# One layer step on one core: the prompt in one pass ahead of the expert gathers, or in groups of 256, 384 and 384 tokens beside them

## The reference, cut to what matters

```python
xn = rmsnorm(x, norm1_w)
q, c, kr, u_pool, gates = mixer_projections(xn, pos, p)   # xn @ w_in, latent norms, rope
attn = prompt_attention(q, c, kr, p)        # 8 heads of 96, causal, keys built from c and kr
# sample: sample_attention(...), online softmax over 32 pages of 128 cached rows per sequence
pool = pool_mix(u_pool, S, p)               # causal means over 2, 4, 8, 16 tokens, then a linear map
mixed = sigmoid(g0) * (attn @ w_attn_br) + sigmoid(g1) * (pool @ w_pool_br)
h = x + mixed @ w_out
y = h + peer(rmsnorm(h, norm2_w), p)
# peer: per token and each of 8 heads, scores against 2 x 128 keys, the best 16 of 16 x 16 sums;
# a = gelu(xn2 . u[e]) for the 128 chosen experts e, y = sum gate * a * v[e]   (u, v: 16384 x 1024)
```

## Time and profile before

| | |
|---|---|
| median of 3 runs | 4643.17 us (4634.75 to 4645.33) |
| profiled execution, its own time | 4673.63 us |
| its span, first to last instruction | 4671.8 us |
| TensorE busy | 3692.4 us, 79% |
| VectorE busy | 2738.3 us, 59% |
| ScalarE busy | 998.0 us, 21% |
| GpSimd busy | 2470.3 us, 53% |
| DMA, all queues | 1306.94 MB |
| first gather | at 1505 us |

### The profile page before, as it was taken

How to read it: one execution, slowest core, us unless ns; L and a number is a source line. 1 busy time by engine, 2 the same in 40 slices (tenths; PEclk the granted TensorE clock), 3 DMA queues, 4 the chain that set the end, 5 groups by cost and what they waited for, 6 DMA issues and landing times.

```text
span 4671.8 us, 47213 instructions
## 1 busy us (share of the span) xinstructions
PE 3692.4 (79%) x13481; PEld 1607.9 (34%) x13481; DVE 2738.3 (59%) x6886; ACT 998.0 (21%) x2045; POOL 2470.3 (53%) x2234
## 2 busy tenths in 40 slices
PE   8998787999998577777877778777878767676556
PEld 4433565444454233333333333333333323230001
DVE  3334331001104878878888888887878765666643
ACT  1121332001200224223323323322322310200000
POOL 0001100000000777777777777777777776677776
PEclk9998878999999788888888888888887878777778
DMA  2002002111323999999999999999999999999999
GB/s 105 1 28 36 2 0 95 41 40 59 109 63 101 361 388 381 396 380 388 396 394 388 388 399 396 392 396 386 396 396 389 374 405 412 386 407 390 372 372 382
DMA packets 441801, 1306.94 MB, mean 280 GB/s; under 512 B 90218, under 2 KB 146923, under 8 KB 438707
## 3 DMA queue, kind: packets, MB, share of 16 engines
q0 software_dynamic: 313344, 1140.99, 62.6%
q1 hardware_dynamic: 128242, 163.51, 10.7%
HBM read 1275.49 MB, written 28.75 MB: 279 GB/s over the span
## 4 chain that ended last, share of the span: by engine, by line
POOL 28%; DMA 14%; PE 11%; issue 10%; DVE 3%; SPq 2%; ACT 1%; DVEq 0%; ACTq 0%; POOLq 0%
POOL arena L1280 28%; DMA arena<-in_peer_v,arena 9%; PE ps_m L1343 4%; PE ps_m L1591 3%; DMA arena<-in_cache_krope 2%; DMA arena<-key_scores 1%; SPq L1544 1%; DMA arena<-in_peer_u,arena 1%; DVE arena L1385 1%; PE ps_m L1581 1%; PE ps_m L1616 1%; PE ps_m L1599 1%; SPq L1542 1%; PE ps_m L1600 1%; PE ps_m L1932 0%
## 5 line engine op out<-in xcount | busy, mean ns | idle before, releaser
L1343 PE MATMUL ps_m<-arena 128*32 128x512 f32 x4352 | 1171.3, 742 | 584.0 <-DMA arena<-in_peer_v,arena 558.3
L1385 DVE CUSTOM_DVE_ANT_0 arena<-arena 128x1024 f32<-128x1024 f32 x1088 | 1318.6, 1225 | 523.1 <-DMA arena<-in_peer_u,arena 491.5
L1280 POOL DMA_INDIRECT arena<-in_peer_u,arena x1088 | 1207.9, 1110 | 639.6 <-issue 329.0
L1280 POOL DMA_INDIRECT arena<-in_peer_v,arena x1088 | 1200.4, 1103 | 403.3 <-issue 306.9
L1343 PEld LDWEIGHTS ps_m<-arena 128*32 128x32 f32 x4352 | 193.8, 120 | 1346.2 <-DMA arena<-in_peer_v,arena 921.5
L1591 PE MATMUL ps_m<-arena 128*128 128x512 f32 x1056 | 567.7, 664 | 2.6 <-ACT arena L1671 2.4
L1581 PE MATMUL ps_m<-const,arena 128*128 128x128 f32 x528 | 135.7, 346 | 177.7 <-DMA arena<-in_cache_krope 148.8
L1591 PEld LDWEIGHTS ps_m<-arena 128*128 128x128 f32 x1056 | 202.5, 213 | 196.9 <-issue 190.5
L1671 ACT ACTIVATE arena<-ps_m 128x512 f32<-128x512 f32 x264 | 158.2, 599 | 514.5 <-PE ps_m L1591 510.0
L944 POOL COPY arena<-arena 128x1024 f32 (+1 forms) x8 | 8.3, 1042 | 489.4 <-POOLq L821 407.4
L1663 ACT ACTIVATE arena<-ps_m 128x256 f32<-128x256 f32 x264 | 101.4, 384 | 689.7 <-PE ps_m L1582 688.7
(11 more groups left out here) (235 smaller groups left out, 4465.4 us busy)
## 6 DMA issues: line engine op xcount, KB each, us to landing
arena<-in_cache_ckv SPq DMA_DIRECT2D x256, 128.0 KB
arena<-in_w_merge SPq DMA_DIRECT2D x16, 1536.0 KB, 9.2
arena<-in_w_peer SPq DMA_DIRECT2D x32, 576.0 KB, 4.1
arena<-in_peer_u,arena POOLq DMA_INDIRECT x1088, 7.6
arena<-in_peer_v,arena POOLq DMA_INDIRECT x1088, 7.6
arena<-key_scores SPq DMA_DIRECT2D x68, 128.0 KB, 10.8
key_scores<-arena SPq DMA_DIRECT2D x32, 256.0 KB, 4.5
arena<-in_w_front SPq DMA_DIRECT2D x1, 4864.0 KB, 18.9
```

Of the source, the lines that this page charges most:

```text
L1280: self.nc.gpsimd.indirect_dma_start(out=ring[:, slot, :], out_offset=None, in_=self.I[table], in_offset=bass.IndirectOffsetOnAxis(ap=self. ...
L1343: mm = self.nc.tensor.matmul(self.acc[32 * j:32 * j + 32, n, :], self.diag[:, (q0 + j) // 16 % DIAGS, (q0 + j) % 16, :], self.v_ring[:, (q ...
L1385: self.nc.vector.tensor_tensor_reduce(out=u, in0=u, in1=self.xrep[jg % self.XBUF], scale=1.0, scalar=0.0, op0=ALU.mult, op1=ALU.add, accum ...
```

## The change

The build keeps one block of instructions. The 1024 prompt tokens are cut into three groups of 2, 3 and 3 tiles of 128 tokens (`GROUPS_OF`). Each engine runs all stages of the first group (with the 64 sample tokens, 320 columns) first; `Now` gives them no slots. Then the gathers start, and the second and third group (384 columns each) are put between the slots by `Main`. Where each piece goes is computed by `Plan`: each piece has an estimated TensorE time, a group has a rate (estimated us per slot, the smallest that lets its scores be ready for `Route`), and `at` and `after` turn a piece into a slot. By its arithmetic group 1 takes the slots from 0 to 197 at a rate of 2.65 and group 2 those from 199 to 432 at 2.4. Page groups start at slot 442, one every 6 slots, the sample tokens' merge at 856, and its last scores are stored by slot 941; SLOTS stays 1108.

```diff
+GROUPS_OF = (2, 3, 3)
-PAGES_AT, PAGE_SLOTS = 16, 12
+PAGE_SLOTS = 6
...
+            pr.sync(Now(sp), groups[0], groups[1])
+            main = Main("SP", sp, ex.sync(sp))
+            for g, following in zip(groups[1:], after[1:]):
+                pr.sync(main, g, following)
+            pg.sync(main)
+            sm.sync(main)
...
+    rate, unit = 2.4, H * tile
+    while True:
+        g = Group(i, tile, tiles, base, rate)
+        if g.half_at <= route_slot(unit) and g.done_at <= route_slot(unit + 4):
+            return g
+        rate += 0.05
...
+    def piece(self, name, us, lead=0):
+        if self.base is None:
+            return
+        self.t += lead
+        self.begin[name] = self.t
+        self.t += us / self.rate
+        self.end[name] = self.t
```

In `Experts`, all four waits for v rows are moved ahead of the products:

```diff
+                for j in range(w):
+                    pe.wait_ge(self.v_in[(q0 + j) % RING], 16 * ((q0 + j) // RING + 1))
                 for n in range(2):
                     for j in range(w):
-                        if n == 0:
-                            pe.wait_ge(self.v_in[(q0 + j) % RING], 16 * ((q0 + j) // RING + 1))
                         mm = self.nc.tensor.matmul(self.acc[32 * j:32 * j + 32, n, :], ...
```

In `Pages`, a page is one transfer of 1152-byte rows from an array that holds both caches, the five steps of a group stand one slot apart, the exponentials stand behind the last page's square, and the weighing stands last:

```diff
-            for cols, src in ((slice(0, KL), "cache_ckv"), (slice(KL + 1, PGW), "cache_krope")):
-                sp.dma_start(self.pages[par][:, j, cols], self.I[src][ds(page, 1)].rearrange("a p c -> (a p) c")).then_inc(self.page_in[par], 16)
+            sp.dma_start(self.pages[par][:, j, 1:PGW], self.I["cache"][ds(page, 1)].rearrange("a p c -> (a p) c")).then_inc(self.page_in[par], 16)
...
             for j in range(5):
-                pe = main.to(slot + 1 + 2 * j)
+                pe = main.to(slot + 1 + j)
                 if gi < DB * GROUPS and j < n:
                     if j + 1 < n:
                         self.transposes(pe, j + 1, at, par)
                     self.keys(pe, j, at, gi, b)
-                if gi and j == 0:
-                    self.spread_maxima(main.to(slot + 2), gi - 1)
-                if gi and j == 2:
+                if gi and j == 1:
+                    self.spread_maxima(pe, gi - 1)
+                if gi and j == 4:
                     self.weigh(pe, self.group(gi - 1)[3], gi - 1, 1 - par)
...
-                if gi and j == 1:
+                if gi and j == 3:
                     self.correct(act, gi - 1)
                     self.exponentials(act, self.group(gi - 1)[3], gi - 1)
```

More of the change, by code:

```diff
@@ L137 @@
[L137 to L147, removed]
-LATT = ATS - 2 * H * NS
-LATE = LATT - 2 * N_IDS
-QT = TOP - H * TOK
-KT = QT - H * TOK
-CT = KT - 2 * TOK
@@ new lines, in _, with route_slot, paced @@
+            pr.vector(Now(dve), groups[0])
+            main = Main("DVE", dve, ex.vector(dve))
+            for g in groups[1:]:
+                pr.vector(main, g)
+            pg.vector(main)
+            sm.vector(main)
+            main.finish()
+def route_slot(unit):
+    return TOPK * (unit - 5) + 4
+def paced(i, tile, tiles, base):
+    if base is None:
+        return Group(i, tile, tiles, None, 1.0)
+    rate, unit = 2.4, H * tile
[4 more added lines that the diff above has]
+        rate += 0.05
+        assert rate < 20
@@ new lines, with __init__, to, finish @@
+class Main:
+    def __init__(self, name, eng, program):
+        self.name, self.eng, self.program, self.at = name, eng, program, 0
+    def to(self, slot):
+        while self.at < slot:
+            next(self.program)
+            self.at += 1
+        return self.eng
+    def finish(self):
+        for _ in self.program:
+            pass
+class Now:
+    def __init__(self, eng):
+        self.eng = eng
+    def to(self, slot):
+        return self.eng
+class Plan:
+    def __init__(self, base, rate):
+        self.base, self.t, self.rate, self.begin, self.end = base, base, rate, {}, {}
+    def piece(self, name, us, lead=0):
[5 more added lines that the diff above has]
+        self.end[name] = self.t
+    def at(self, name, part=0.0):
+        if self.base is None:
+            return 0
+        return int(self.begin[name] + part * (self.end[name] - self.begin[name]))
+    def after(self, name, more=0):
+        if self.base is None:
+            return 0
+        return int(self.end[name]) + 1 + more
@@ new lines, in act_scores @@
+    def act_scores(self, main, g):
+        s, ps, i, T = self.nc.scalar, self.ps, g.i, g.T
+        for j in range(2 * H):
+            n = 16 * i + j
+            if g.first and j >= 10 and j % 2 == 0:
+                self.rt.softmax(main.to(0), j // 2 - 5)
+            act = main.to(g.after(f"s{j}") - 1)
+            act.wait_ge(self.q_done, n + 1)
+            if j >= 2:
+                act.wait_ge(self.k_done, n - 1)
+            s.activation(self.qb(g, j % 2), ps[:, 2 + j % 2, 0:T], ACT.Copy).then_inc(self.q_out, 1)
@@ L1798, in vector @@
     def vector(self, main):
-        main.to(PAGES_AT)
+        main.to(self.first)
         self.start_batch()
```

2217 lines of the change are left out of this document (1205 added, 1012 removed).

## The result

The changed kernel takes 4725.82 us (median of 4 runs, 4721.13 to 4750.06) where the kernel before takes 4644.25 (4 runs beside it, 4634.75 to 4660.01): a ratio of 1.0183, with an interval from 1.0137 to 1.0228. The forecast was 4695 us and slower; the range was 4370 to 4980. The profiled execution took 4721.1 us with a span of 4719.1.

The account below looks back on a forecast made before the run. TensorE bounds the front and transfers the rest, in balance with a closed page loop that would bind after the change; 405 + 1560 + 1978 + 335 + 448 = 4726 us of span, 4695 us as median, range 4370 to 4980.

Parts of the forecast that it names:

- front: Work before the gathers: 312 us of TensorE work and 93 us that no work covers, 405 us (370 to 440).
- first groups: Slots 0 to 442, prompt groups 1 and 2: gathers plus reread weights plus 3%, 1560 us (1450 to 1860).
- pages: Slots 442 to 852: 64 page groups at 30.3 us, new rows and first load, 1978 us (1790 to 2220).
- The factor to the median: Step from profiled span to median of the runs: 0.9935, taking 4726 us to 4695 us.
- The sign: Whole kernel: slower, 4695 against 4643 us; faster 0.39 with A and B, slower 0.56 with C.
- rival C: Slots 0 to 442: prompt groups fall behind at 4.2 us a slot, 1856 us there, 4990 us in all; 20%.
- The page loop: Page stage: closed loop of 21.8 us to the weighing's end, 0.8 and 7.7 of load, 30.3 us a group.
- half-rate restart: First keys of each page group after the DMA wait: low clock, 3.41 us against 1.72, penalty 1.7 us a group.
- The four waits: Waits for second rows ahead of the products, 272 blocks: up to 54 us lost or 40 gained, taken as 0.
- Rival D: Expert product blocks: the wait for four rows is what counts, 54 us either way at most; no chance given.
- A: Whole kernel: transfers bind throughout at a DMA share of 1.01, median 3860 us; 5%.
- B: Page stage: the loop closes in 25 us, pages landing 5 us after first issue, median 4340 us, faster; 17%.

Follow-up runs that it names:

- the first experiments: Changed kernel with TensorE's waits for second rows back between the products, 4803.1 us; kernel before with all four waits ahead of the products, 4877.92 us.
- the changed kernel with the waits between: Changed kernel with TensorE waiting for each second row just before its own product, not for all four ahead: 4803.1 us, on another chip 4718.05 us.
- the last version: Changed kernel with three page buffers, maxima one slot later, page numbers read before the wait, second-row waits between products, exponentials before the last page's square: 4074.87 us.
- the third buffer: Changed kernel with three buffers for page groups instead of two, so a load may start two groups ahead: 4349.87 us, on another chip 4310.93 us.
- edits worth 453 and 311 us alone: Changed kernel with a third page buffer, 4349.87 us, or with the weighing of a page group two slots earlier, 4491.61 us; both together 4301.58 us.
- kernel before with four waits: Kernel before with TensorE waiting for all four second rows of a block ahead of its eight products: 4877.92 us, ratio 1.0052.

## Why the prediction was right

**The frame.** The sum of five parts was 4726 us of span, and 4719.1 were measured. No part is off by more than 53 us. That the whole is off by only 7 is luck, since +77 and -84 cancel: front +24 (by the first dot product; the first gather is issued at 382 where about 390 was named), first groups -32, pages +53, sample -33, tail -19. The reading on which it rests is that the front's transfers and TensorE's page loop are what the moved work meets, not the busy shares.

**The factor to the median** was the larger error in the number. The profiled execution of before was slow among its own runs (0.9935 of it is the median); that of after was the fastest of its four (4721.1, median 4725.8), so the factor was not one of the program. Taking 0.9935 over to after cost 31 us, which is all of the distance from 4695 to 4726.

**The sign** held by little. 36 and 20 per cent stood on slower, 39 on faster, and on the chip of the first experiments the sign is the other one: there the changed kernel with the waits between takes 0.988 of the kernel before.

**Slots 0 to 442.** 3.43 us a slot were worked out and 3.46 measured, DMA share 0.96. The 328 us for the groups' weights at 3.2 us a MB and the 3 per cent for waits in order were enough; rival C, 4.2 us a slot, has nothing in the trace: TensorE is busy 81% there and waits 108 us in all for v rows and 37 for score weights.

**The page loop.** 30.3 us were built from rows of before and 31.4 measured. TensorE's section from restart to the weighing's end is 21.9 us in the mean of the chain (19.1 to 25.4; 23.5 in the group shown), where 21.8 were worked out. The load from there to the restart is 9.6 us in the mean (6.9 to 11.9), where 8.5 were worked out. So the term that was mis-sized is the load: SP's fourth issue comes 4.1 us after the weighing, as in the sum (0.8 + 3.3), but the restart then comes 5.5 us later, where 4.4 were left for it. Of the two reasons that the forecast gave for a shorter load, fewer issues are confirmed (two transfers a page cost 2.3 us more up to the last issue) and fewer descriptors are not: with 1024 instead of 512 the landing is 5.3 us. What brought the landing down from the 10.3 us in the earlier trace rows is then most likely the queue that is no longer full (DMA share 0.67 for 1.01), which no run varies alone.

The Trainium skill (TensorE: Matmul & The Clock Gate, HAM oscillation) was brought in for the half-rate restart. Of 62 restarts after a wait for pages, the first keys take 2.3 to 3.4 us in 58 and 1.96 in four, 2.9 in the mean, where the keys behind them take 1.72; the sum had 3.41 in every round. When the wait for pages is taken out the granted clock of the stretch rises from 0.82 to 0.90 with the buffer and 0.95 in the last version. The trace agrees with that rule; the penalty is part of what a wait for a DMA costs in each round, beside the wait itself.

**The four waits** were taken as nothing, from -40 to +54 us. Measured: 8 us between two medians, within noise, and 8 to 42 in the kernel before. Rival D was no cause, and the clock that it hoped to keep fell.

**The rivals.** A (transfers bind throughout) is ruled out by a DMA share of 0.67. B (a loop of 25 us) had the right place: the loop closes near 25 us once the load leaves it. That the time worked out for B, 4340 us, is nearly what the third buffer measured (4311 and 4350 us) is chance, because B keeps the load in the loop. It asked for pages that land 5 us after the first issue; the last lands 9.3 us after it in the group shown, and 8.9 in the mean. The turning point that B names, 29.3 us a group, is 29.5 by the forecast's own terms; nothing else hangs on it.

What the forecast did not see is what stands behind the load. It took TensorE's section as the remainder. The runs showed more waits in TensorE's round, hidden by the load before: for VectorE's norms and maxima (some 2 us a group, of which 0.8 came back when it was taken out), and for ScalarE's exponentials (1.7 us, of which 1.2 went in the last version). A group takes 31.4 us, then 23.9 to 24.4, 23.1 and 21.0 as they are opened one after the other; the last step isn't taken apart.

## What to carry to other kernels

Where neither an engine nor the DMA engines are full, look for a circle: restart, last use, load, restart. Its time doesn't shrink with the number of slots given to it, and a fixed amount of work per round turns into lost time for everything that was meant to run beside it, here 834 us, of which 661 went when the waits were taken out (2031 to 1370 us). Count buffers by the distance from a load to the last use and not to the first: with the weighing one group late, two buffers leave none to load ahead, and a third (1156 words of a partition) was worth 9 per cent. And when one loop is opened, expect the next at once and ask for its length before adding up gains: edits worth 453 and 311 us alone were worth 425 together (on another chip, where the time of a group says the same: 24.4 and 26.7 alone, 24.7 together).

## What the runs showed of the hardware

The kernel before isn't the same on all chips: 4645, 4647, 4817 and 4867 us on four of them, 4.8 per cent, while kernels of the changed kind move by 1.8 (4718 and 4803 us with the waits between; on these two chips the ratio to the kernel before is 1.016 and 0.988, so which of the two is faster depends on the chip). In the kernel before with four waits, on the slowest, a page group takes 38.4 us instead of 35.2, at a granted clock of 0.78 for 0.83 and a DMA share of 0.95 for 1.01 between 1505 and 3760 us (part of the lower clock is that of the four waits, see above):

```profile
L1604 PE MATMUL ps_m<-const,arena x64: 272/421/424, 1563.1 to 3981.3; 128*64 128x128 f32 x64
```

```profile
1505.00:3760.00 2255.00, 1479.62 (x6625) 699.75 (x6625) 1677.44 (x4457) 592.55 (x1308) 1572.13 (x1448) 0.78 0.95 357
```

The front is untouched by it (1351.7 us of TensorE in 1505, for 1367.7 in the earlier trace rows), so it isn't TensorE's speed. What differs is what the gathers move. Here is the end, where they run alone and no page group does, in the kernel before on the first chip and, with four waits, on the slowest:

```profile
4271.00:4631.00 360.00, 218.26 (x522) 34.53 (x523) 203.71 (x449) 11.65 (x24) 280.79 (x261) 0.77 0.99 380
```

```profile
4486.00:4846.00 360.00, 132.97 (x496) 25.91 (x496) 192.30 (x411) 11.04 (x21) 266.68 (x247) 0.63 0.97 361
```

380 GB/s there and 361 here. One and the same kernel, the changed one with the waits between, moves 393 GB/s at its end on one chip and 370 on the slowest:

```profile
4396.00:4756.00 360.00, 222.47 (x511) 33.94 (x512) 197.19 (x427) 11.26 (x22) 270.02 (x252) 0.74 0.98 370
```

Its stretches there are 3 us shorter (front), then 29, 36, 9 and 24 us longer (slots 0 to 442, 442 to 852, 852 to 941, the rest: 452 for 428 us). So on such a chip the gathers are 5 to 6 per cent slower where they run alone. The kernel before is bound by transfers for 3167 us, the changed one only outside its page loop, which fits the larger loss of the first. In the page stages of the kernel before the loss is larger still, 7 to 9 per cent by the run with four waits; what adds to it there, and why the gathers of those chips are slower, no run tells.
